# The last attention of a three-mixer network: from a stage behind its input GEMM to blocks of four heads between the weight slabs

## The reference, cut to what matters

```python
proj = h @ w_in                                  # 1024 -> 3*3*1024 + 1024
for g, (window, dilation) in enumerate(DILATED_GROUPS):
    q = rms_norm_2(qkv[:, :, g, 0], q_gain[g])   # over the 64 of a head
    k = rms_norm_2(qkv[:, :, g, 1], k_gain[g])
    o, l = dilated_group_attention(q, k, qkv[:, :, g, 2], bias_g, window, dilation)
alpha = jax.nn.softmax(jnp.stack(lses, axis=0), axis=0)
o = jnp.sum(alpha[..., None] * jnp.stack(outs, axis=0), axis=0)
y = o.reshape(B, S, ATTN_WIDTH) * jax.nn.silu(z)
return y @ w_out
```

## Time and profile before

| | us |
|---|---|
| median of 3 runs (2275.89 to 2277.4) | 2276.96 |
| span of the profiled execution, first to last instruction | 2279.6 |
| PE busy (share) | 2034.0 (89%) |
| DVE busy | 1248.6 (55%) |
| ACT busy | 912.0 (40%) |
| POOL busy | 74.7 (3%) |
| mean granted clock of TensorE, share of 2.4 GHz | 0.885 |

### The profile page before, as it was taken

How to read it: one execution, slowest core, us unless ns; L and a number is a source line. 1 busy time by engine, 2 the same in 40 slices (tenths; PEclk the granted TensorE clock), 3 DMA queues, 4 the chain that set the end, 5 groups by cost and what they waited for, 6 DMA issues and landing times.

```text
span 2279.6 us, 28042 instructions
## 1 busy us (share of the span) xinstructions
PE 2034.0 (89%) x11307; PEld 1692.7 (74%) x11307; DVE 1248.6 (55%) x2096; ACT 912.0 (40%) x1213; POOL 74.7 (3%) x135
## 2 busy tenths in 40 slices
PE   4799868868999999989967789987999899999998
PEld 2678656556777777868845569976999698888887
DVE  3453376653666655455356657765666554545443
ACT  4434512222544444343452235554334455664221
POOL 0000000021000000010000100001000000000000
PEclk9899976769999999989968799998999999997557
DMA  7534100002344552324400045544666455545331
GB/s 247 183 129 157 65 1 1 1 1 93 111 148 148 159 164 84 101 89 145 133 19 1 1 157 177 188 145 131 186 187 186 161 151 168 177 160 127 39 31 37
DMA packets 211455, 261.42 MB, mean 115 GB/s; under 512 B 4657, under 2 KB 173283, under 8 KB 211071
## 3 DMA queue, kind: packets, MB, share of 16 engines
q1 hardware_dynamic: 207690, 248.34, 33.7%
q0 software_dynamic: 3232, 11.15, 3.0%
q10 hardware_dynamic: 405, 0.15, 0.0%
HBM read 258.50 MB, written 1.12 MB: 114 GB/s over the span
## 4 chain that ended last, share of the span: by engine, by line
PE 64%; issue 13%; DVE 12%; ACT 5%; DMA 5%; POOL 1%; SPq 0%; DVEq 0%; ACTq 0%; POOLq 0%
PE acc L625 15%; PE acc L627 14%; PE acc L626 14%; PE acc L1068 3%; PE acc L1091 3%; DVE scratch L1785 3%; PE acc L799 2%; PE acc L655 2%; PE acc L656 2%; PE acc L1080 2%; DVE weights_low L1618 2%; ACT weights_high L1230 1%; DMA weights<-in_w_up_dram 1%; DVE mixer_scratch L1766 1%; DVE scratch L1766 1%
## 5 line engine op out<-in xcount | busy, mean ns | idle before, releaser
L1618 DVE TENSOR_TENSOR weights_low<-weights,weights_high 128x2048 fp32r<-128x2048 f32 x232 | 526.7, 2273 | 587.4 <-ACT weights_high L1230 587.2
L1230 ACT ACTIVATE weights_high<-weights 128x2048 fp32r<-128x2048 f32 x232 | 440.0, 1899 | 611.7 <-DMA weights<-in_w_ada_dram 119.7
L625 PE MATMUL acc<-normed_t_high,weights_high 128*128 128x256 f32 (+1 forms) x1824 | 577.0, 316 | 5.6 <-DVE weights_low L1618 3.0
L626 PE MATMUL acc<-normed_t_low,weights_high 128*128 128x256 f32 (+1 forms) x1824 | 564.6, 310 | 0.0
L627 PE MATMUL acc<-normed_t_high,weights_low 128*128 128x256 f32 (+1 forms) x1824 | 563.6, 309 | 0.0
L625 PEld LDWEIGHTS acc<-normed_t_high,weights_high 128*128 128x128 f32 x1824 | 346.5, 190 | 36.8 <-issue 6.2
L626 PEld LDWEIGHTS acc<-normed_t_low,weights_high 128*128 128x128 f32 x1824 | 343.8, 189 | 22.8 <-issue 3.8
L627 PEld LDWEIGHTS acc<-normed_t_high,weights_low 128*128 128x128 f32 x1824 | 344.0, 189 | 20.8
L625 PE MATMUL acc<-weights_high,normed_t_high 128*128 128x512 f32 (+1 forms) x792 | 313.6, 396 | 28.2 <-DVE normed_t_low L1926 27.8
L626 PE MATMUL acc<-weights_low,normed_t_high 128*128 128x512 f32 (+1 forms) x792 | 309.7, 391 | 0.0
L627 PE MATMUL acc<-weights_high,normed_t_low 128*128 128x512 f32 (+1 forms) x792 | 309.5, 391 | 0.0
(11 more groups left out here) (216 smaller groups left out, 2248.0 us busy)
## 6 DMA issues: line engine op xcount, KB each, us to landing
weights<-in_w_ada_dram SPq DMA_DIRECT2D x48, 1024.0 KB, 5.3
weights<-in_w_up_dram SPq DMA_DIRECT2D x44, 1024.0 KB, 6.4
weights<-in_attn_w_in_dram SPq DMA_DIRECT2D x40, 1024.0 KB, 5.1
weights<-in_conv_w_in_dram SPq DMA_DIRECT2D x32, 1024.0 KB, 5.8
weights<-in_w_in_dram SPq DMA_DIRECT2D x24, 1024.0 KB, 6.5
weights<-in_w_down_dram SPq DMA_DIRECT2D x20, 1024.0 KB, 5.0
weights<-in_w_out_dram SPq DMA_DIRECT2D x8, 1024.0 KB, 5.0
weights<-in_conv_w_out_dram SPq DMA_DIRECT2D x8, 1024.0 KB, 5.0
```

The lines of the kernel that those rows point to most:

```text
L625: pe.matmul(o, ah, bh, start=start, stop=False)
L626: pe.matmul(o, ah, bl, start=False, stop=False)
L1230: act.activation(hi_slot(n)[:, 0:used], slot(n)[:, 0:used], ACT.Copy).then_inc(hi_in.sem, 1)
L1618: dve.tensor_tensor(slot(n, ring_lo)[:, 0:used], slot(n)[:, 0:used], hi_slot(n)[:, 0:used], ALU.subtract).then_inc(lo_in.sem, 1)
```

## The change

1. The slabs of `A_IN` are ordered by block j of four heads: for g in 0..2: q, k, v of these heads; after the four blocks of nine slabs the four z slabs. `QKEYS` follows. The v slabs are now 256 columns x all rows, 48 products with 256 columns each, and one PSUM group for both token tiles; one copy by ACT per slab.
2. `attend(st)`, the former loop body on PE, ACT and DVE, is called by `STEPS_AFTER`: block j's eight units one behind each of the first eight slabs of block j+1 (slabs 9 to 16, 18 to 25, 27 to 34); the last block's units two behind each z slab; three more steps drain the pipeline. On ACT and DVE the call stands behind `split_next()` of the same slab. A block's first unit waits on PE for the last scaled k and the v copies of its block.
3. The mean is copied from PSUM by ACT (`take_mean`) and Ln reads the copy; batches are of three keys, two per block.
4. z is only copied, behind the last q/k scaling; one Silu over all of `ZS` stands ahead of the three drain steps.
5. `SQ`, `RQ` and `Y2` move to other buffers (the unused halves of the normed input and the residual), as the units' scratch is now live at the same time.

```diff
-        QKEYS = [(g, a, j) for g in range(NG) for a in range(2) for j in range(4)]
+        HB = 4
+        QKEYS = [(g, a, j) for j in range(HB) for g in range(NG) for a in range(2)]
...
+        A_IN = [(g, a, j) for j in range(HB) for g in range(NG) for a in range(3)]
         A_IN += [("z", 0, j) for j in range(4)]
         for g, a, j in A_IN:
-            if a == 2:
-                by_rows(("a_in", g, a, j), W, 512 * (j % 2), 4, g * 3072 + 2048 + 512 * (j // 2))
-            else:
-                by_columns(("a_in", g, a, j), W, (NG * 3072 if g == "z" else g * 3072 + a * 1024) + 256 * j)
+            by_columns(("a_in", g, a, j), W, (NG * 3072 if g == "z" else g * 3072 + a * 1024) + 256 * j)
+        UNITS_B = 2 * NH // HB
+        STEPS_AFTER = {n: [] for n in range(len(A_IN))}
+        for j in range(HB - 1):
+            for i in range(UNITS_B):
+                STEPS_AFTER[9 * j + 9 + i].append(UNITS_B * j + i)
+        for i in range(UNITS_B):
+            STEPS_AFTER[9 * HB + i // 2].append(UNITS_B * (HB - 1) + i)
+        LAST_STEPS = [len(BU), len(BU) + 1, len(BU) + 2]
```

On PE:

```diff
+            def attend(st):
                 if st < U:
                     h, t = BU[st]
+                    if st % UNITS_B == 0:
+                        j = st // UNITS_B
+                        pe.wait_ge(q_done.sem, q_done.after((NG - 1, 1, j)))
+                        for g in range(NG):
+                            pe.wait_ge(*taken_after(("v2", g, j)))
...
+                else:
+                    wh, wl = halves(w, KT)
+                    o = open_group(("v2", g, j))
+                    for t in range(2):
+                        cs = slice(256 + t * P, 256 + (t + 1) * P)
+                        for k in range(KT):
+                            last = product(o[:, 256 * t:256 * t + 256], (HH[:, k, cs], HL[:, k, cs]), (wh[:, k, :], wl[:, k, :]),
+                                           k == 0, k == KT - 1)
+                    last.then_inc(full, 1)
+                release()
+                if len(pend) > 1 or (a == 2 and pend):
+                    mean_of(pend.pop(0))
+                for st in STEPS_AFTER[i]:
+                    attend(st)
+            for st in LAST_STEPS:
+                attend(st)
```

On ACT:

```diff
+            def take_mean(key):
+                n = QKEYS.index(key)
+                act.wait_ge(full, full_after(("ms", key)))
+                if n >= 4:
+                    act.wait_ge(q_done.sem, q_done.after(QKEYS[n - 4]))
+                act.activation(RQ[:, n % 4, :], bank(("ms", key)), ACT.Copy).then_inc(taken_of(("ms", key)), 1)
...
+                    act.activation(SQ[n % 2], bank(("qk", key)).rearrange("p (k n) -> p k n", k=2), ACT.Square, scale=0.125).then_inc(q_sq.sem, 1)
+                    pend.append(key)
+                    if a:
+                        take_mean((g, 0, j))
+                    if len(pend) == 4:
+                        scales_of(pend[:3])
+                        pend = pend[3:]
+                else:
...
+                    take_mean((g, 1, j))
+                    if g == NG - 1:
+                        scales_of(pend)
+                        pend = []
+                if i < len(A_IN) - 1:
+                    split_next()
+                for st in STEPS_AFTER[i]:
+                    attend(st)
+            for k in range(4):
+                act.wait_ge(*taken_after(("z2", k)))
+            act.activation(ZS, ZS, ACT.Silu).then_inc(z_silu, 1)
+            for st in LAST_STEPS:
+                attend(st)
```

On DVE:

```diff
+                if i < len(A_IN) - 1:
+                    split_next()
+                for st in STEPS_AFTER[i]:
+                    attend(st)
+            for st in LAST_STEPS:
+                attend(st)
+            dve.wait_ge(z_silu, 1)
```

More of the change, by code:

```diff
@@ L300, in program @@
         s_hot = sem("hot_in")
+        z_silu = sem("z_silu")
         s_bias = [sem(f"bias_in{i}") for i in range(3)]
@@ L1023, in mean_of @@
                 o = open_group(("ms", key))
[L1024 to L1058, removed]
+                pe.matmul(o[:, :], means, SQ[QKEYS.index(key) % 2], start=True, stop=True).then_inc(full, 1)
@@ L1059, in _ @@
             U = len(BU)
-            for st in range(U + 3):
+            def attend(st):
                 if st < U:
                     h, t = BU[st]
+                    if st % UNITS_B == 0:
[3 more added lines that the diff above has]
+                            pe.wait_ge(*taken_after(("v2", g, j)))
                     r = slice(64 * (h % 2), 64 * (h % 2) + 64)
@@ L1093, in _ @@
                     last.then_inc(full, 1)
+            for i, (g, a, j) in enumerate(A_IN):
+                w = weights(("a_in", g, a, j))
+                if g == "z":
+                    t_out(("z2", j), w, 0, slice(256, 512), close_=False)
+                    t_out(("z2", j), w, 1, slice(256, 512), 256, open_=False)
+                elif a < 2:
+                    key = (g, a, j)
+                    t_out(("qk", key), w, 0, slice(256, 512), close_=False, normed=("an", 0) if i == 0 else None)
+                    t_out(("qk", key), w, 1, slice(256, 512), 256, open_=False)
+                    pend.append(key)
[15 more added lines that the diff above has]
+                attend(st)
             for u in range(U - 8, U):
@@ L1098, in _ @@
                 for t in range(2):
-                    last = pe.matmul(o[:, t * P:(t + 1) * P], Y2[:, t, k * P:(k + 1) * P], flip, start=True, stop=True)
+                    last = pe.matmul(o[:, t * P:(t + 1) * P], Y2[:, k, t, :], flip, start=True, stop=True)
                 last.then_inc(full, 1)
@@ L2077, in scale, with attend @@
                     dve.tensor_tensor(q_place(key), q_place(key), r, ALU.mult).then_inc(q_done.sem, 1)
-            for g, a, j in A_IN:
-                if g != "z" and a < 2:
-                    key = (g, a, j)
-                    dve.wait_ge(q_sq.sem, q_sq.after(key))
-                    dve.tensor_scalar(q_place(key), bank(("qk", key)).rearrange("p (m n) -> p m n", m=4), pcol(("gain", a), g), None,
-                                      ALU.mult).then_inc(taken_of(("qk", key)), 1)
-                    dve.wait_ge(*taken_after(("qk", key)))
-                    pend.append(key)
-                    if len(pend) == 5:
-                        scale(pend[:4])
-                        pend = pend[4:]
-                elif a == 2 and j == 0:
-                    scale(pend)
-                    pend = []
-                if (g, j) != ("z", 3):
-                    split_next()
-            for st in range(len(BU) + 3):
+            def attend(st):
                 if st < len(BU):
@@ L2135, in _ @@
                     dve.wait_ge(full, full_after(("o2", u)))
-                    dve.tensor_scalar(Y2[:, t, h * 64:(h + 1) * 64], bank(("o2", u), 64), brec[:, b:b + 1], None,
+                    dve.tensor_scalar(Y2[:, h // 2, t, h % 2 * 64:h % 2 * 64 + 64], bank(("o2", u), 64), brec[:, b:b + 1], None,
                                                       ALU.mult).then_inc(taken_of(("o2", u)), 1)
+            for i, (g, a, j) in enumerate(A_IN):
+                if g != "z" and a < 2:
+                    key = (g, a, j)
+                    dve.wait_ge(q_sq.sem, q_sq.after(key))
+                    dve.tensor_scalar(q_place(key), bank(("qk", key)).rearrange("p (m n) -> p m n", m=4), pcol(("gain", a), g), None,
+                                      ALU.mult).then_inc(taken_of(("qk", key)), 1)
+                    dve.wait_ge(*taken_after(("qk", key)))
+                    pend.append(key)
+                    if len(pend) == 4:
+                        scale(pend[:3])
+                        pend = pend[3:]
+                elif g == NG - 1:
+                    scale(pend)
+                    pend = []
+                if i < len(A_IN) - 1:
[5 more added lines that the diff above has]
+            dve.wait_ge(z_silu, 1)
             for k in range(KT):
```

67 lines of the change are left out of this document (28 added, 39 removed).

## The result

The changed kernel takes **2303.2 us** (median of 4 runs, 2298.3 to 2310.0) against 2276.6 for the kernel before, a ratio of 1.0122 [1.0102, 1.0141]: slower by 27 us, where 30 were forecast. The profiled execution has a span of 2308.2 us, 28.6 more than before. Of these 2.9 lie ahead of the first product of the stage (now at 1831.7 us), in code that the change leaves alone, 27.6 between that product and the flip of `Y2`, and -1.8 behind it.

What follows compares the result with a forecast made beforehand. PE bounds GEMM and attention, the latter at half clock; after the change a load-split-softmax chain would. 60.3 + 282.1 + 78.9 = 421.3 us against 415.5, taken as +1, plus 29 for clock falls: 2277.0 becomes 2307 us, range 2255 to 2335.

Steps and rivals of the forecast that it cites:

- The wait that takes the place of the removed one: GEMM steps with units: softmax behind the load-bound split, copies at T + 13.4, two 256-key steps 20.9 us against PE's 18.2.
- One sign of the prediction: ACT in the attention: its wait for DVE's row maxima, 116 us before, would be gone if the forecast was right.
- The slab order, V's shape and the copied means: GEMM: V slabs 6.1 us; 24 added ACT mean copies, 0.6 each, in ACT's gaps except in the batches.
- PE's own work: Last stage on PE alone: 347 us against 415.5, with slabs 6.1, units 2.6, first nine slabs 60.3.
- POOL's bias loads: Beside weight loads in the GEMM: delay them at worst in 128-key steps, which have 2 us of room.
- The clock: PE pauses amid the GEMM: nine counted as falls, six half, 2.5 us per slab; 29 us in all.
- that rival: GEMM steps with units: clock falls in every step, 3.8 us over some eleven pairs, +63, 2340 us; chance 0.10.
- the z part: Last block's units, two behind each z slab: steps 21.2, 18.8, 18.8 us, end at 78.9 before clock costs.
- a batch of scales: Step of slab 9j+4: ACT does 7.5 us before its split, copies 18.9 after T, PE stands 4.4 us.
- The sum: Last stage: 421.3 us against 415.5, taken as +1, plus 29 for the clock: +30 us, 2307 us.

Runs made afterwards that it cites:

- experiment 4: Changed kernel with only DVE taking its part of the unit ahead of the split, ACT's order kept: 2237.1 us, ratio 0.9841.
- experiment 2: Changed kernel's slab order, 256-wide V slabs, mean copies and single Silu, but all units behind the GEMM as before: 2276.7 us, ratio 1.0011.
- experiment 1: Changed kernel with the unit's part ahead of the split of slab i+3 on both ACT and DVE: 2240.8 us, ratio 0.9842.
- experiment 11: Changed kernel without the bias loads of heads 3 to 15, which reuse those of heads 0 to 2: 2295.1 us, ratio 1.0088.
- experiment 5: Changed kernel with fourteen extra dense products ahead of the transposes in ten 128-key steps: 2306.3 us, ratio 1.0140.
- experiments 5 and 10: The second of these: changed kernel with the first's fill, plus bias loads held until the next weight load has landed: 2302.6 us, ratio 1.0111.

## Why the prediction was right, step by step

**The wait that takes the place of the removed one: shown.** The times in the step of slab 19 are those of the prediction within 0.3 us (+5.3, +7.4, copies at +13.4), two steps take 23.8, 23.7 and 21.9 us (slabs 19 to 25) in the forecast's 20 to 24 and 23.5 to 23.7 in the third block (in the first 16.2, 22.7 and 24.5, with the first units and the long loads in it), PE's idle time stands at the transposes behind ACT's copy. Taking DVE's part of the unit out from behind the split gives back some 65 us (experiment 4). One sign of the prediction failed: ACT's wait for the maxima stayed, 123 us, though its own chain has 2.5 us to the maximum in every 256-key unit. The slab order, V's shape and the copied means, costed at nothing, are that within a few us (experiment 2).

**PE's own work: right where it could be seen.** Two steps of experiment 1 take 17.8 to 18.8 us where 18.2 were worked out. Two terms were high: a slab behind a unit at full clock takes 5.8, not 6.1, and the first nine slabs 56.7, not 60.3.

**POOL's bias loads: costed at nothing, measured about 8 us.** The step that failed was "delay them at worst in the 128-key steps, which have 2 us of room". The delay per meeting is 4.5 to 5.2 us, which no step has, and it adds to the chain, since the split waits for the load (experiment 11).

**The clock: the sum near, its premise wrong.** The forecast counted eight of the 24 slabs behind units as cold, for 15.5 us; 11 were, for 19.1. It had expected few and long pauses; there are many of 1.6 to 2.2 us, and the clock fell behind nearly all of them. The premise that failed is the one drawn from the earlier trace rows: a pause of 1.6 us had held 1.00 there, amid dense products alone; here such pauses stand beside the unit's thin fp32 passes. That the thin passes are what makes the difference no run shows. The prediction weighed that row against the Trainium skill, TensorE: Matmul & The Clock Gate, section "A second HAM failure mode: psum-queue depth-cycling". By that rule a fall in every pair of steps was to be expected, "some eleven pairs", and in how often the clock fell this trace sides with it: 11 cold slabs. The price of a fall was near what that rival took, too: a cold slab lost 0.9 to 2.2 us (2.5 taken) and the value passes of the second and third block took 2.2 to 2.7 us for 1.45 (1.3 more taken); a pair took 3.2 us longer than with the fill of experiment 5, where 3.8 were taken. That it was not 2340 has other reasons: the first nine slabs and the z part were costed 3.6 and 6.4 us too high, and in the step of a batch of scales a cold slab costs nothing, since PE would have waited for ACT's copies anyway (0.4 us of wait in the changed kernel, 2.4 and 0.8 with the fill). In the z part the pieces erred the other way: 92.4 us were forecast with the clock (78.9 and 13.5), 86.0 measured. The steps of its last two slabs took 20.3 and 20.4 us where 18.8 and 3.15 were taken, and that of the second 22.7 where 21.2, 3.15 and 2.5 were, as its cold slabs lost 1.4 each.

**The sum.** From first product to flip 445.5 us were forecast and 443.0 measured, but misses cancel in it: the 8 us of bias loads and the larger clock loss in the blocks against the shorter z part and the shorter start. The number was thus partly luck. Nor do clock and chain simply add up, as in the prediction. In a pair of steps between batches they do (20.6 us without the fall, 23.8 with it), but experiments 5 and 10 kept the clock up there and the end did not move: the next batch took part of the gain back as a wait, the fills have a price of their own, and in experiment 5 two loads met. How much of the 27 us the clock alone accounts for therefore stays open. Shown is that the place of DVE's part of the unit accounts for all 27 and more, and the bias loads for about 8 of them. That the chain of a batch of scales sets its step whatever PE gained before is read from the traces (copies 18.5 to 18.7 us behind the end of slab 22 in the changed kernel and in experiments 5 and 10); a run without a batch was not tried.

## What to carry to other kernels

When work is threaded into a loop whose operands come through a ring, ask of each in-order engine what it does first: the refill of a slot, which waits for a load that starts only now, must stand behind the work whose consumer is next, or the loop runs at the pace of load plus split plus that work. Filling PE's pauses held the clock and shortened the steps here, and the program took as long as before: before you count such a gain, ask which wait comes next and whether it swallows it. Small loads from another queue deserve a price of their own where a tight chain waits for a large load that starts just behind them.

## What the runs showed of the hardware that was not expected

- A 1 MB weight load issued 1 to 2 us behind a 384 KB load of another queue landed after 9.6 to 10.3 us in place of 5.1, twice the time for 1.4 times the bytes; without the bias loads none that ACT waited for took over 5.2 (experiment 11).
- At full clock the fourteen 256-wide products take 1.94 us; issued just behind a pause of 1.7 us that follows thin fp32 passes, 3.29 us.
- The same sort of pause (1.6 to 2.2 us) ended in a fall to 0.50 between fp32 passes of 64 to 512 columns, eight times of nine in the three blocks, while one of 1.6 us amid dense products alone did not the earlier trace rows.
